# Gates of a gated recurrence: 64-row products with both gates side by side in place of block-diagonal 128-row products

## Chip, cores and metric

One core of a Trainium2 chip runs the whole program. The metric is the device time in microseconds (us) of one execution; lower is better.

## What is computed

One step of a one-layer hybrid decoder over 512 prompt positions and 8 x 4 sample positions (544 tokens). Three branches (GLA, mLSTM, RG-LRU) are fed from one input projection, gated and summed; a convolutional feed-forward part follows. The change touches the gates of the RG-LRU branch only:

```python
def blockdiag(x, w):
    nb, bs, _ = w.shape
    xb = x.reshape(x.shape[:-1] + (nb, bs))
    return jnp.einsum('blnd,nde->blne', xb, w).reshape(x.shape)

# R_WIDTH = 512, R_BLOCKS = 8, so w_rglru_r and w_rglru_i are (8, 64, 64)
r_g = sigmoid(blockdiag(xc, w_rglru_r) + b_rglru_r)
i_g = sigmoid(blockdiag(xc, w_rglru_i) + b_rglru_i)
log_a = R_C * r_g * log_sigmoid(lam)
a = exp(log_a)
bx = sqrt(-expm1(2 * log_a)) * (i_g * xc)
# h[t] = a[t] * h[t-1] + bx[t];   o_r = h * gelu(ry)
```

## The kernel before

Channels lie on partitions, tokens along the free axis. The 512 channels of the RG-LRU branch are four blocks of 128 (i = 0 to 3), and each of them holds two of the 64-channel blocks of the gate weights. A block's row is 568 elements long (512 prompt positions and eight samples with the convolution's padding between).

**The order of the work.** TensorE works through "units": unit u multiplies one 1024 x 128 tile of a weight matrix by all tokens (48 matmuls of 272 columns, L605; each weight is split into a high part `whi` and a low part `wlo`, so three passes). For each unit SyncE loads `stage`, ScalarE copies it into `whi` (L1078), GpSimd subtracts to make `wlo` (L545); ScalarE also copies the unit's product out of PSUM (`gg`, `mo` and others: L1160, L1163). Between the units every engine makes "visits", small pieces of the recurrences, in an order written out by hand in a table (`plan`). Block i of the RG-LRU is `rg` on TensorE and ScalarE and `rgd` on VectorE, behind units 23, 24, 26 and 27; `gfin` (`gv`, `ogh`, `ogl`) stands between block 1 and block 2 on VectorE. TensorE starts unit u only when the product of unit u - 2 has been copied out, and all of them by the end of unit 28, when the gate units begin.

**A block's chain.** VectorE convolves `rx` into `rt[i % 2]` (L1534, L1536, in four steps). TensorE makes the products (L796): `bd` is [128, gate, block, 128], two 64 x 64 gate blocks on the diagonal and zeros beside them. Per block there are four products, two gates times two halves of 284 columns, each into a bank of its own from 4 to 7. ScalarE takes the sigmoid of both gates with their bias from `par` (L1272, L1273), then tanh, exp and sqrt (L1277 to L1279), with two table loads between. VectorE multiplies, scans and multiplies by `ry` (L1816 to L1826, `rg_o`), and splits the result into `orh` and `orl` (L1829, L1830). ScalarE's next block waits for `rg_o` of this one; TensorE's next products wait for this one's sigmoids (`rg_copied`) and for the convolution (`xc`). In ScalarE's queue the next unit's `whi` and copy-out stand behind a block's square root, and GpSimd's `wlo` waits for the `whi`.

**Around it.** `bd` is filled with zeros by GpSimd at the start (L552); SyncE waits for that before it loads the four diagonal parts. `par`, the per-channel biases and gains, is copied out of PSUM by VectorE in two pieces (L1576, L1577), and `cst` is a small tile of 8 columns, of which four are used.

Of the kernel before, what the change touches and what calls it, by code (L numbers as in the profile page):

```python
# [25 lines left out]
ACT = mybir.ActivationFunctionType  # L26
X = mybir.AxisListType.X

P = 128
# [10 lines left out]
CW, FW = 4, 3  # L40
# [21 lines left out]
CONVM = PADM - (CW - 1)  # L62
# [24 lines left out]
P_G2, P_GG, P_MG, P_MCW, P_MCB, P_RCW, P_RCB, P_BR, P_BI, P_LAM = 52, 60, 64, 68, 84, 88, 104, 108, 112, 116  # L87
# [35 lines left out]
def layer(nc, io):  # L123
    ctx = ExitStack()
    with ctx:
        sems = {}

        def s(name):
            if name not in sems:
                sems[name] = ctx.enter_context(nc.semaphore("s_" + name))  # L130
            return sems[name]
# [4 lines left out]
        def at(name, shape, off, dt=F32):  # L136
            return nc.alloc_sbuf_tensor_at(name, shape, dt, offset=BASE + off)
# [13 lines left out]
        o = 71680  # L151
        ident = at("ident", [P, P], o)
        ones = at("ones", [P, P], o + 512)
        par = at("par", [P, PAR_N + KD], o + 1024)
        cst = at("cst", [P, 8], o + 2304)
# [34 lines left out]
        rx = at("rx", [P, 4, PADM], o)  # L190
# [6 lines left out]
        pm = at("pm", [P, 4, PADM], o)  # L197
# [19 lines left out]
        rt = [at(f"rt{i}", [P, PADM], w0 + 12288 + (i + 4) % 6 * 2304) for i in range(6)]  # L217
# [18 lines left out]
        sel = at("sel", [4, H, P], o + 2336)  # L236
        wa2 = at("wa2", [RANK, 2 * P], o + 4384)
        wq = at("wq", [P, 3, H, P], o + 5408)
        bd = at("bd", [P, 2, 4, P], o + 11552)
        ch = at("ch", [P, NB, P], o + 11552)  # L240
        cols = at("cols", [P, 5, 100], o + 15648)
        ecol = at("ecol", [P, 5, 68], o + 17664)
# [61 lines left out]
        def split(ap):  # L304
            return ap.rearrange("p (a b) -> p a b", a=2)
# [3 lines left out]
        def bank(i):  # L309
            return ps[:, i * 512:(i + 1) * 512]  # L310
# [73 lines left out]
        def _(sp):  # L384
# [61 lines left out]
            for n, name in enumerate(("w_mlstm_q", "w_mlstm_k", "w_mlstm_v")):  # L446
                sp.dma_start(wq[:, n], io[name][0].rearrange("h d e -> d h e")).then_inc(s("wq_in"), 16)
            load_all(U_RX, tiles(w_in, C_RX, 8), 8)
            sp.wait_ge(s("zeroed"), 1)
            for n, name in enumerate(("w_rglru_r", "w_rglru_i")):  # L450
                for r in range(2):
                    src = io[name][0].rearrange("(t r) d e -> r d t e", r=2)[r]
                    sp.dma_start(bd[64 * r:64 * r + 64, n, :, 64 * r:64 * r + 64], src).then_inc(s("bd_in"), 16)
            load_all(U_GG, tiles(w_in, C_GG, 4), 4)
            load_all(U_MO, tiles(w_in, C_MO, 4), 4)

# [57 lines left out]
            sem, value = used(U_DOWN - 1)  # L514
# [13 lines left out]
        @block.gpsimd  # L528
        def _(pool):
            done = [0]  # L530

            def then(ins):

                done[0] += 1
                ins.then_inc(s("pool_step"), 1)
                pool.wait_ge(s("pool_step"), done[0])

            def pick(t, op, fill, base, pattern, mult):
                return pool.affine_select(out=t, in_=t, compare_op=op, fill=fill, base=base, pattern=pattern,
                                          channel_multiplier=mult)  # L540

            def lo(u, slot, kt):

                pool.wait_ge(s("hi"), u + 1)
                pool.tensor_tensor(wlo[:, slot, 0:kt], stage[:, slot, 0:kt], whi[:, slot, 0:kt].bitcast(F32),  # L545
                                   ALU.subtract).then_inc(s("lo"), 1)

            then(pool.memset(ident[:], 0.0))
            pick(ident[:], ALU.not_equal, 1.0, 0, [[-1, P]], 1).then_inc(s("ident"), 1)
            for area, value in ((bd[:], 0.0), (ones[:], 1.0), (pm[:, :, 0:CW - 1], 0.0), (rx[:, :, 0:CW - 1], 0.0),  # L550
                                (gst[:], 0.0)):
                pool.memset(area, value).then_inc(s("zeroed"), 1)  # L552
            pool.wait_ge(s("hi"), 1)
            pool.tensor_tensor(wlo[:, 0, :, 0:N_SMALL], stage[:, 0, :, 0:N_SMALL], whi[:, 0, :, 0:N_SMALL].bitcast(F32),
                               ALU.subtract).then_inc(s("lo"), 1)
            lo(1, 1, KT)
            pool.wait_ge(s("lo"), 2)
            pool.memset(qz[0:64, :, 1, :], 0.0).then_inc(s("zeroed"), 1)
            pool.memset(qz[64:P, :, 0, :], 0.0).then_inc(s("zeroed"), 1)
            pool.wait_ge(s("zeroed"), 7)  # L560

            for t, v, fill in ((negm, 0.0, NEG), (cau, 1.0, 0.0)):
                then(pool.memset(t[:], v))
                pick(t[:], ALU.is_ge, fill, 0, [[1, P]], -1).then_inc(s("masks"), 1)
            for t, v, fill in ((negs, 0.0, NEG), (caus, 1.0, 0.0)):
                view = t[:].rearrange("p (b t) -> p b t", t=LS)
                then(pool.memset(t[:], v))
                then(pick(view, ALU.is_ge, fill, 0, [[LS, NB], [1, LS]], -1))
                pick(view, ALU.is_ge, fill, 0, [[-LS, NB], [0, LS]], 1).then_inc(s("masks"), 1)

            then(pool.memset(blk[:], 1.0))
            then(pick(blk[:], ALU.is_ge, 0.0, 0, [[-LS, NB]], 1))
            pick(blk[:], ALU.is_ge, 0.0, LS - 1, [[LS, NB]], -1).then_inc(s("masks"), 1)

            then(pool.memset(blkc[:], 0.0))
            pick(blkc[:].rearrange("p a (b t) -> p a b t", t=LS), ALU.not_equal, 1.0, 0,
                 [[1, NB], [-1, NB], [0, LS]], 0).then_inc(s("masks"), 1)

            then(pool.memset(sel[:], 0.0))
            pick(sel[:], ALU.not_equal, 1.0, 0, [[-1, H], [0, P]], 1).then_inc(s("masks"), 1)  # L580

            lo(2, 2, KT)
            for u0, u1 in ((SLOTS, U_DVE), (U_DOWN, U_END)):
                with pool.Fori(0, (u1 - u0) // SLOTS) as i:
                    for r in range(SLOTS):
                        lo(i * SLOTS + (u0 + r), (u0 + r) % SLOTS, kt_of(u0 + r))

        @block.tensor
        def _(pe):
            mm = nc.tensor.matmul  # L590
# [193 lines left out]
            def v_rg(i):  # L784

                pe.wait_ge(s("xc"), i + 1)
                if i == 0:
                    pe.wait_ge(s("bd_in"), 64)
                    pe.wait_ge(s("ss_new"), 2)
                    pe.wait_ge(s("state_rows"), 2)  # L790
                else:
                    pe.wait_ge(s("rg_copied"), i)
                for w in range(2):
                    for r in range(2):
                        n = CONVM // 2
                        ins = mm(bank(4 + 2 * w + r)[:, 0:n], bd[:, w, i, :], rt[i % 2][:, r * n:(r + 1) * n],  # L796
                                 start=True, stop=True)
                ins.then_inc(s("rg_mm"), 1)

# [182 lines left out]
            for b in range(NB):  # L982
                g, q = divmod(b, FST_BANK)
                ins = tr(bank(4 + g)[:, q * NFR:(q + 1) * NFR], fraw[:, b, :], NFR)
# [3 lines left out]
            for r in range(2):  # L988
                ins = mm(halves(3)[:, r, :], ones[:], ssa[:, r * HT:(r + 1) * HT], start=True, stop=True)
# [29 lines left out]
            for m in range(2):  # L1019
                pe.wait_ge(s("uev"), 2 * NF - 1 + m)  # L1020
                down(m, m, hidden=m == 0)
                if m == 0:
# [4 lines left out]
                    for b in range(1 + NB):  # L1027
                        ins = tr(ps[0:NFR, 2048 + b * P:2048 + (b + 1) * P], rows[:, b * NFR:(b + 1) * NFR], P)
# [18 lines left out]
            for t in range(5):  # L1047
                n = P if t < 4 else TS
                ins = mm(bank(4)[0:n, t:t + 1], yss[:, t * P:t * P + n], ones[:, 0:1], start=True, stop=True)
# [3 lines left out]
        def _(act):  # L1053
            func = nc.scalar.activation
# [211 lines left out]
            def v_rg(i):  # L1266
                act.wait_ge(s("rg_mm"), i + 1)
                if i:
                    act.wait_ge(s("rg_o"), i)
                c0 = CONVM // 2  # L1270
                v = [pair(2 + w).rearrange("p (a b) -> p a b", a=2)[:, :, 0:c0] for w in range(2)]
                func(rt[2][:, 0:CONVM].rearrange("p (a b) -> p a b", a=2), v[0], ACT.Sigmoid, bias=par[:, P_BR + i:P_BR + i + 1])  # L1272
                func(rt[3][:, 0:CONVM].rearrange("p (a b) -> p a b", a=2), v[1], ACT.Sigmoid, bias=par[:, P_BI + i:P_BI + i + 1])\  # L1273
                    .then_inc(s("rg_copied"), 1)
                act.wait_ge(s("rg_copied"), i + 1)
                act.wait_ge(s("c4"), 1)
                then(func(rt[4][:, 0:CONVM], rt[2][:, 0:CONVM], ACT.Tanh, scale=c4[:, i:i + 1]))  # L1277
                func(rt[2][:, 0:CONVM], rt[2][:, 0:CONVM], ACT.Exp, scale=lz[:, i:i + 1])
                func(rt[4][:, 0:CONVM], rt[4][:, 0:CONVM], ACT.Sqrt).then_inc(s("rg_u"), 1)  # L1279
# [122 lines left out]
            for n in range(2 * KD):  # L1402
                u = U_GB + n
                g = PB_GATE + GATE_OF[n // KD] * KD + n % KD
                i, r = divmod(n, 2)
# [20 lines left out]
            for r in range(2):  # L1426
                i = KD // 2 - 1
# [94 lines left out]
        def _(dve):  # L1522
# [48 lines left out]
                v.scalar_tensor_tensor(out=xl[:, j, :], in0=pair(XN_PAIR[j])[:, 0:T], scalar=par[:, P_G1 + j:P_G1 + j + 1],  # L1571
                                       in1=xh[:, j, :].bitcast(F32), op0=ALU.mult, op1=ALU.subtract).then_inc(s("xl"), 1)

            dve.wait_ge(s("zeroed"), 7)
            dve.wait_ge(s("par_tr"), 2)
            v.tensor_copy(par[:, 0:P_LAM + 4], bank(4)[:, 0:P_LAM + 4])  # L1576
            v.tensor_copy(par[:, P:PAR_N], bank(4)[:, P:PAR_N]).then_inc(s("par"), 1)  # L1577
            dve.wait_ge(s("par_tr"), 3)
            for w, dst in enumerate((pm, rx)):
# [592 lines left out]
```

## Time and profile before

| | |
|---|---|
| Median of 3 runs | 1024.71 us (1024.48 to 1026.93) |
| The profiled execution | 1024.34 us |
| Its span, first to last instruction | 1022.3 us |
| TensorE busy | 979.2 us (96%) |
| VectorE busy | 563.2 us (55%) |
| ScalarE busy | 425.0 us (42%) |
| GpSimd busy | 248.2 us (24%) |
| Mean granted TensorE clock | 0.983 |

The profile is of one execution. Busy times are sums over an engine's own instructions; engines work side by side, so the busiest is near the span and the others are not added to it. What lies around the span (2.0 us) belongs to the time but not to the trace.

### The profile page before, as it was taken

Reading aid. Unit: us, or ns where it says so; the run is one execution under the profiler, and the core shown is the slowest. Engines: PE = TensorE matmul, PEld = TensorE weight load, DVE = VectorE, ACT = ScalarE, POOL = GpSimd, SP = SyncE. Lnnn points to the kernel's source line nnn. Section 1 sums busy time; section 2 is a strip of 40 time slices with the busy share of each in tenths; the row PEclk is TensorE's granted clock in tenths of the full one; section 3 lists DMA queues with packets and bytes.
Section 4 is the critical chain, followed back from the end, with each engine's and each line's share of the span. In section 5 each row is a group of like instructions: output and inputs, shape, how many; then the busy total and the mean of one; then the engine's idle time right before and its main releaser. Section 6 shows DMA issues by size and latency. Waiting matters only on the chain.

```text
span 1022.3 us, 19012 instructions
## 1 busy us (share of the span) xinstructions
PE 979.2 (96%) x7594; PEld 953.9 (93%) x7594; DVE 563.2 (55%) x1007; ACT 425.0 (42%) x578; POOL 248.2 (24%) x129
## 2 busy tenths in 40 slices
PE   7999999985899999999999999999999999999995
PEld 6999999884899999888999999999999999999995
DVE  4486336449743345447334577777777777412122
ACT  5642332484544455222232345544554554222221
POOL 3543222313132222222353320000000001334340
PEclk9999999996999999999999999999999999999998
DMA  6243422232122223424421522223322321522212
GB/s 178 71 125 87 109 73 68 67 82 62 42 63 84 63 62 104 121 66 128 135 85 38 139 83 83 83 82 91 94 82 83 100 84 56 141 87 85 84 38 88
DMA packets 159982, 89.38 MB, mean 87 GB/s; under 512 B 6404, under 2 KB 158050, under 8 KB 159929
## 3 DMA queue, kind: packets, MB, share of 16 engines
q1 hardware_dynamic: 144928, 79.16, 27.0%
q10 hardware_dynamic: 15000, 9.47, 3.2%
q8 instruction: 39, 0.64, 0.3%
q14 instruction: 15, 0.12, 0.0%
HBM read 82.29 MB, written 6.32 MB: 87 GB/s over the span
## 4 chain that ended last, share of the span: by engine, by line
PE 84%; DVE 9%; ACT 3%; issue 2%; DMA 0%; ACTq 0%; DVEq 0%
PE ps L605 73%; PE ps L594 4%; PE ps L898 1%; PE ps L817 1%; PE ps L902 1%; PE ps L613 1%; DVE rt L1818 1%; DMA xtok<-x_prompt 0%; PE ps L836 0%; PE ps L832 0%; DVE rt L1822 0%; PE ps L843 0%; DVE omh L1947 0%; PE ps L773 0%; ACT whi L1078 0%
## 5 line engine op out<-in xcount | busy, mean ns | idle before, releaser
L545 POOL TENSOR_TENSOR wlo<-stage,whi 128x1024 fp32r<-128x1024 f32 (+1 forms) x98 | 237.6, 2426 | 733.8 <-ACT whi L1078 733.7
L605 PE MATMUL ps<-xh,whi 128*128 128x272 f32 x1536 | 323.4, 292 | 8.4 <-ACT mo L1163 8.4
L605 PE MATMUL ps<-xh,wlo 128*128 128x272 f32 x1536 | 319.0, 289 | 0.0
L605 PE MATMUL ps<-xl,whi 128*128 128x272 f32 x1536 | 318.2, 289 | 0.0
L605 PEld LDWEIGHTS ps<-xh,whi 128*128 128x128 f32 x1536 | 243.4, 190 | 11.3 <-ACT mo L1163 9.1
L1078 ACT ACTIVATE whi<-stage 128x1024 fp32r<-128x1024 f32 x140 | 146.3, 1045 | 236.9 <-PE ps L605 230.8
L605 PEld LDWEIGHTS ps<-xl,whi 128*128 128x128 f32 x1536 | 243.1, 190 | 0.0
L605 PEld LDWEIGHTS ps<-xh,wlo 128*128 128x128 f32 x1536 | 241.4, 190 | 0.0
L2049 DVE SCALAR_TENSOR_TENSOR ca<-up,par,ca 128x560 f32<-128x560 f32 x88 | 74.1, 842 | 7.6 <-DVE ca L2049 2.7
L605 PE MATMUL ps<-hh,whi 128*128 128x272 f32 x352 | 73.6, 291 | 0.0
L605 PE MATMUL ps<-hl,whi 128*128 128x272 f32 x352 | 72.7, 288 | 0.0
L605 PE MATMUL ps<-hh,wlo 128*128 128x272 f32 x352 | 72.6, 287 | 0.0
L2096 DVE TENSOR_TENSOR yb<-xt,ps 128x544 f32<-128x544 f32 x8 | 5.8, 721 | 106.7 <-PE ps L605 106.7
L605 PEld LDWEIGHTS ps<-hl,whi 128*128 128x128 f32 x352 | 55.6, 188 | 0.0
L605 PEld LDWEIGHTS ps<-hh,wlo 128*128 128x128 f32 x352 | 55.0, 188 | 0.0
L605 PEld LDWEIGHTS ps<-hh,whi 128*128 128x128 f32 x352 | 54.9, 188 | 0.1
L2056 DVE TENSOR_TENSOR wlo<-stage,whi 128x1024 fp32r<-128x1024 f32 x42 | 51.4, 1223 | 0.9 <-ACT whi L1078 0.2
L1400 ACT ACTIVATE sg<-ps,par 128x544 f32<-128x544 f32 x24 | 17.1, 714 | 82.6 <-PE ps L605 77.5
L1449 ACT ACTIVATE hh<-hp 128x512 f32 (+1 forms) x22 | 13.9, 633 | 70.4 <-DVE hp L2078 70.4
L1460 ACT ACTIVATE ca<-up,par 128x560 f32<-128x560 f32 x44 | 37.6, 855 | 6.2 <-DVE up L2032 5.7
L1971 DVE TENSOR_TENSOR sg<-sg,ps 128x544 f32<-128x544 f32 x16 | 11.5, 719 | 49.3 <-PE ps L605 47.3
L1455 ACT ACTIVATE ca<-ca 128x560 f32<-128x560 f32 x22 | 14.8, 672 | 49.9 <-DVE ca L2049 49.9
(416 smaller groups left out, 1324.4 us busy)
## 6 DMA issues: line engine op xcount, KB each, us to landing
stage<-w_in SPq DMA_DIRECT2D x52, 512.0 KB, 3.7
stage<-w_up SPq DMA_DIRECT2D x44, 512.0 KB, 3.7
stage<-w_down SPq DMA_DIRECT2D x16, 512.0 KB, 4.0
stage<-w_branch SPq DMA_DIRECT2D x12, 512.0 KB, 3.3
stage<-w_out SPq DMA_DIRECT2D x8, 512.0 KB, 4.1
stage<-w_down SPq DMA_DIRECT2D x8, 384.0 KB, 3.4
ch<-state_mlstm_C ACTq DMA_DIRECT2D x4, 512.0 KB, 4.9
s_mlstm_C<-ch ACTq DMA_DIRECT2D x4, 512.0 KB, 3.2
```

Of the source, the lines that this page charges most:

```text
L545: pool.tensor_tensor(wlo[:, slot, 0:kt], stage[:, slot, 0:kt], whi[:, slot, 0:kt].bitcast(F32), ALU.subtract).then_inc(s("lo"), 1)
L594: return nc.tensor.transpose(out, in_, ident[0:k, 0:k])
L605: ins = mm(dst[:, r, :], w[:, slot, k0 + step * k, :], x(k)[:, r * HT:(r + 1) * HT], start=first and k == 0 and q == 0, stop=last and k == ...
L613: ins = mm(small_out[0:N_SMALL, c0:c1], w[:, 0, k, 0:N_SMALL], x[:, k, c0:c1], start=k == 0 and q == 0, stop=k == KD - 1 and q == 2)
L1078: func(whi[:, slot, 0:kt], stage[:, slot, 0:kt], ACT.Copy).then_inc(s("hi"), 1)
L1400: func(split(sg[:]), halves(0), ACT.Sigmoid, bias=col).then_inc(s("gate_ev"), 1)
L1449: func(dst[:, 0:SEQ], hp[:, 0:SEQ], ACT.Copy)
L1455: func(ca[:, 0, 0:CONVF], ca[:, 0, 0:CONVF], ACT.Gelu_apprx_tanh).then_inc(s("gelu"), 1)
L1460: func(ca[:, r, 0:CONVF], up[:, r, 0:CONVF], ACT.Identity, bias=par[:, bass.ds(j + (P_FB + NF * r), 1)], scale=par[:, bass.ds(j + (P_FW + ...
L1971: v.tensor_tensor(split(sg[:]), split(sg[:]), halves(1), ALU.mult).then_inc(s("br_mul"), 1)
L2049: v.scalar_tensor_tensor(out=out, in0=row[:, k:k + CONVF], scalar=w, in1=out, op0=ALU.mult, op1=ALU.add)\
L2056: v.tensor_tensor(wlo[:, slot], stage[:, slot], whi[:, slot].bitcast(F32), ALU.subtract).then_inc(s("lo_up"), 1)
```

## The change

Two 64 x 64 gate blocks no longer stand on a diagonal with zeros beside them. `bd` becomes [128, block, 128]: on each half of the partitions both gates of one 64-channel block stand side by side. On partitions 0 to 63 the r gate has columns 0 to 63 and the i gate 64 to 127; on partitions 64 to 127 it is the other way round. A product takes 64 rows of weights and gives both gates of 64 channels. The four products of a block stand in the order (half of the columns, half of the channels). Since a product's result holds one gate on its lower and one on its upper 64 partitions, ScalarE takes the sigmoids in four activations of 64 partitions, and for the i gate it reads one half of the partitions and writes the other. The i gate's bias must lie on the partitions that are read, so VectorE makes a copy of it with the halves exchanged, in `cst` columns 4 to 7. The zero fill and its wait go.

```diff
-        bd = at("bd", [P, 2, 4, P], o + 11552)
+        bd = at("bd", [P, 4, P], o + 11552)
...
-            sp.wait_ge(s("zeroed"), 1)
             for n, name in enumerate(("w_rglru_r", "w_rglru_i")):
                 for r in range(2):
                     src = io[name][0].rearrange("(t r) d e -> r d t e", r=2)[r]
-                    sp.dma_start(bd[64 * r:64 * r + 64, n, :, 64 * r:64 * r + 64], src).then_inc(s("bd_in"), 16)
+                    c0 = 64 * (n ^ r)
+                    sp.dma_start(bd[64 * r:64 * r + 64, :, c0:c0 + 64], src).then_inc(s("bd_in"), 16)
...
-            for area, value in ((bd[:], 0.0), (ones[:], 1.0), (pm[:, :, 0:CW - 1], 0.0), (rx[:, :, 0:CW - 1], 0.0),
+            for area, value in ((ones[:], 1.0), (pm[:, :, 0:CW - 1], 0.0), (rx[:, :, 0:CW - 1], 0.0),
                                 (gst[:], 0.0)):
...
-            pool.wait_ge(s("zeroed"), 7)
+            pool.wait_ge(s("zeroed"), 6)
...
-                for w in range(2):
-                    for r in range(2):
-                        n = CONVM // 2
-                        ins = mm(bank(4 + 2 * w + r)[:, 0:n], bd[:, w, i, :], rt[i % 2][:, r * n:(r + 1) * n],
+                for r in range(2):
+                    for b in range(2):
+                        n, q = CONVM // 2, slice(64 * b, 64 * b + 64)
+                        ins = mm(bank(4 + 2 * b + r)[:, 0:n], bd[q, i, :], rt[i % 2][q, r * n:(r + 1) * n],
                                  start=True, stop=True)
                 ins.then_inc(s("rg_mm"), 1)
...
-                func(rt[2][:, 0:CONVM].rearrange("p (a b) -> p a b", a=2), v[0], ACT.Sigmoid, bias=par[:, P_BR + i:P_BR + i + 1])
-                func(rt[3][:, 0:CONVM].rearrange("p (a b) -> p a b", a=2), v[1], ACT.Sigmoid, bias=par[:, P_BI + i:P_BI + i + 1])\
-                    .then_inc(s("rg_copied"), 1)
+                for b in range(2):
+                    q, other = slice(64 * b, 64 * b + 64), slice(64 - 64 * b, P - 64 * b)
+                    func(split(rt[2][q, 0:CONVM]), v[b][q], ACT.Sigmoid, bias=par[q, P_BR + i:P_BR + i + 1])
+                    ins = func(split(rt[3][q, 0:CONVM]), v[b][other], ACT.Sigmoid, bias=cst[other, 4 + i:5 + i])
+                ins.then_inc(s("rg_copied"), 1)
...
-            dve.wait_ge(s("zeroed"), 7)
+            dve.wait_ge(s("zeroed"), 6)
             dve.wait_ge(s("par_tr"), 2)
             v.tensor_copy(par[:, 0:P_LAM + 4], bank(4)[:, 0:P_LAM + 4])
+            for b in range(2):
+                v.tensor_copy(cst[64 - 64 * b:P - 64 * b, 4:8], bank(4)[64 * b:64 * b + 64, P_BI:P_BI + 4])
             v.tensor_copy(par[:, P:PAR_N], bank(4)[:, P:PAR_N]).then_inc(s("par"), 1)
```

On ScalarE, at block 0 of the RG-LRU (`rt_115` to `rt_117` are `rt[2]` to `rt[4]`; - is before, + is the changed kernel; its line numbers stand two higher from here on):

```order
-L1272 ACT_TABLE_LOAD
-L1272 ACTIVATE rt_115<-ps,par 128x568
-L1273 ACTIVATE rt_116<-ps,par 128x568
-L1277 ACTIVATE rt_117<-rt_115,sml 128x568
+L1274 ACT_TABLE_LOAD
+L1274 ACTIVATE rt_115<-ps,par 64x568
+L1275 ACTIVATE rt_116<-ps,cst 64x568
+L1274 ACTIVATE rt_115<-ps,par 64x568
+L1275 ACTIVATE rt_116<-ps,cst 64x568
+L1279 ACTIVATE rt_117<-rt_115,sml 128x568
```

Two more activations stand ahead of the tanh; the table loads and the rest of the block stay in their places, in the other three blocks too.

On TensorE nothing moves: the four products of a block (now L796 with 64 rows of weights) stand between the same units. On VectorE the two copies of the exchanged bias stand between those into `par`:

```order
L1578 COPY par<-ps 128x120
L1580 COPY cst<-ps 64x4 x2
L1581 COPY par<-ps 128x178
```

Before, nothing stood between the two copies into `par`.

## Rows read from the trace of the kernel before

**Rows 1.** The page: busy tenths and granted clock in 40 equal slices.

```profile
PE   7999999985899999999999999999999999999995
PEclk9999999996999999999999999999999999999998
```

**Rows 2.** Waits of TensorE, 200 to 270 us: total, times, longest us.

```profile
PE ps L796 <- DVE rt L1536: 11.0, 2, 10.3
PE ps L605 <- ACT mo L1163: 8.4, 2, 4.3
```

**Rows 3.** Chain of waits, 180 to 300 us: start us, us, what.

```profile
188.77 6.02 PE ps L605 x48
...
222.55 0.74 ACT rt L1272
...
238.85 2.87 DVE gv L1791 x4
...
250.59 0.75 DVE rt L1816
...
255.42 0.07 ACT rt L1272
```

**Rows 4.** Timeline of TensorE: start us, us, operation, count [idle before]; blocks 0 and 3.

```profile
202.74 2.08 PE L796 MATMUL ps<-rt,bd 128*128 128x284 f32 x8
204.44 0.62 PE L605 MATMUL ps<-xh,whi 128*128 128x272 f32 x2
...
250.60 3.76 PE L796 MATMUL ps<-rt,bd 128*128 128x284 f32 x8 [10.31 <-DVE rt L1536]
```

**Rows 5.** The same timeline, a 64-row product and what follows it.

```profile
194.71 1.98 PE L773 MATMUL ps<-vb,kz 64*128 64x512 f32 x4
196.62 0.52 PE L605 MATMUL ps<-xh,whi 128*128 128x272 f32 x2
```

**Rows 6.** Groups of instructions by form, ScalarE: shapes, count | busy us, mean ns.

```profile
L1231 ACT ACTIVATE ot<-ps 128x512 f32<-128x512 f32 x4 | 2.4, 602 | 0.0
...
L1246 ACT ACTIVATE rout<-ps 27x512 f32<-27x512 f32 x2 | 1.2, 580 | 0.7 <-ACT rout L1246 0.7
```

**Rows 7.** Timeline of ScalarE, block 0.

```profile
208.09 0.73 ACT L1272 ACTIVATE rt<-ps,par 128x568 f32<-128x568 f32 x1
208.72 0.73 ACT L1273 ACTIVATE rt<-ps,par 128x568 f32<-128x568 f32 x1
209.48 0.77 ACT L1277 ACTIVATE rt<-rt,sml 128x568 f32<-128x568 f32 x1
```

**Rows 8.** Timeline of ScalarE, neighbours that read different partitions.

```profile
173.13 0.37 ACT L1234 ACTIVATE ot<-ps 32x256 f32<-32x256 f32 x1 [2.88 <-PE ps L760]
...
173.52 0.38 ACT L1234 ACTIVATE ot<-ps 32x256 f32<-32x256 f32 x1
```

**Rows 9.** Timelines of GpSimd and VectorE before block 2, and L1534 by form.

```profile
245.03 2.67 POOL L545 TENSOR_TENSOR wlo<-stage,whi 128x1024 fp32r<-128x1024 f32 x1 [9.72 <-ACT whi L1078]
...
245.42 2.60 DVE L1534 TENSOR_SCALAR rt<-rx,par 128x568 f32<-128x568 f32 x1
...
L1534 DVE TENSOR_SCALAR rt<-pm,par 128x568 f32<-128x568 f32 x4 | 2.3, 571 | 0.0
```

**Rows 10.** Timeline of TensorE behind two waits; a window's row ends clock, DMA, GB/s.

```profile
231.79 0.82 PE L605 MATMUL ps<-xh,whi 128*128 128x272 f32 x2 [4.12 <-ACT mo L1163]
...
236.87 0.41 PE L605 MATMUL ps<-xh,wlo 128*128 128x272 f32 x2
...
264.67 0.82 PE L605 MATMUL ps<-xh,whi 128*128 128x272 f32 x2 [4.29 <-ACT mo L1163]
...
267.53 0.41 PE L605 MATMUL ps<-xh,whi 128*128 128x272 f32 x2
...
265.00:266.00 1.00, 1.00 (x6) 1.00 (x6) 0.95 (x3) 0.00 (x0) 0.30 (x1) 0.50 0.00 0
```

**Rows 11.** Timeline of VectorE and the chain of waits, start of the program.

```profile
28.40 0.33 DVE L1577 COPY par<-ps 128x178 f32<-128x178 f32 x1
...
35.21 2.02 PE ps L684 x8
```

## Prediction

> **What bounds the kernel now.** The page comes first. TensorE (PE) is busy 96% of the span and its granted clock is near full in all slices but one [rows 1], so over most of the program only TensorE time counts. The tenth slice, from about 230 to 256 us, is the exception (PE busy 5 tenths, clock 6 tenths), and the edited code stands just there. The second view, the waits of TensorE from 200 to 270 us, says how it idles: 11.0 us for the convolution that VectorE makes (L1536) and 8.4 us for ScalarE's `mo` copy-out (L1163) [rows 2], 19.4 us together. The third view, the chain of waits of that stretch, says what sets its length. It is not TensorE. From block 0's sigmoid on, at 208.09 us, the chain goes ScalarE, VectorE, ScalarE, VectorE through the four blocks of the gate recurrence and comes back to TensorE only at 264.67 us [rows 3]: block 0 on ScalarE and VectorE, then block 1 on ScalarE and VectorE, then VectorE's `gv`, `ogh`, `ogl` and the convolution for block 3, VectorE's share of block 2, then ScalarE for block 3, the `whi` copy, a table load and `mo`, for which TensorE waits. Only ScalarE's share of block 2 is off the chain: VectorE starts that block's first step at 250.59 us, straight behind the convolution.
>
> **The products.** Before, each block has four fp32 products over 128 rows of weights, half of them zeros. In block 0 they take 1.70 us from their start to the next unit's (202.74 to 204.44 us), and in block 3 3.76 us, at the lower clock [rows 4]. The number of products stays at four and so does their column count, 284; what falls is the rows, from 128 to 64, with neighbours in the order now on different halves of the array. No row here shows two 64-row products side by side, so their saving is bounded: nothing below, and half above, 0.85 us in each of three blocks at the full clock and 1.9 us in block 3, 4.4 us over all four. I cost it at nothing, whichever it is. In blocks 0 and 1 what hides it is the ScalarE and VectorE chain: TensorE works ahead there and then waits for the convolution [rows 2]. In block 3 ScalarE starts its sigmoid at 255.42 us, after VectorE's L1826, while the products ended at 250.60 + 3.76 = 254.36 us [rows 3, 4]: even unshortened they leave 1.1 us. If this cover were gone, the 4.4 us would be the rival below. A 64-row product between 128-row ones exists already (L773), and what follows it starts 1.91 us later, with no gap around it [rows 5], so switching itself costs nothing that shows. The Trainium skill, TensorEngine Tiling (Array Packing), section Key Properties, says that changing the tiling mode drains TensorE; that speaks against the change, but the rows around L773 leave less than 0.1 us for it, and the sum would be the same by it, as TensorE is idle later in any case.
>
> **The sigmoids: the term that counts.** Two activations of 128 partitions become four of 64 partitions, each over the same 568 elements. ScalarE's time goes with the elements of a partition and not with the partitions: 27x512 takes 580 ns, 128x512 takes 602 ns [rows 6]. So each of the four costs what one costs now, 0.73 us. In the trace the second sigmoid starts 0.63 us after the first and the tanh 0.76 us after the second, 1.39 us from the first sigmoid to the tanh [rows 7]. What two more add depends on whether neighbours still overlap by 0.1 us. If they do, each adds 0.63 us, 1.26 us a block. The only pair in this trace of which the second reads other partitions than the first is L1234's: 0.37 us long, and the second starts 0.39 us after the first [rows 8], so no overlap. In the new code each of the four differs from its neighbour in the start partition of its input or its output. By L1234's row the steps are 0.75 us: three of them and the last 0.76 us are 3.0 us, against 1.39 us, so **+1.6 us a block**. I take that, since it is the pair that has the same trait. The Trainium skill, ScalarE: Activation LUTs, section What ACT_TABLE_LOAD costs, gives back-to-back ACTIVATEs an overlap of about 93 ns and makes no exception; by it each block would pay 1.3 us and the sum below would be 0.9 us less. The table loads stay as they are.
>
> Blocks 0, 1 and 3 have this on the chain: 3 x 1.6 = **+4.8 us**. In block 2 ScalarE's part is done before 245.03 us, when GpSimd's `wlo`, which follows the copy behind that block's square root, starts [rows 9]. Late by three blocks' worth it is done before 249.8 us, while VectorE comes to it at 250.59 + 3.2 = 253.8 us. Hidden there, with 4.0 us left.
>
> **What the shift meets.** VectorE's operations that read SBUF stand still while GpSimd's `wlo` subtraction runs. At that 245.03 us `wlo` starts, and VectorE's L1534, 0.57 us when free, takes 2.60 us [rows 9]. `wlo` moves by 4.8 us (to 249.8 us), but VectorE's convolution, by 3.2 us (to 248.6 us). So it is caught one step later, in the second or third of its four steps. It pays about the same, 2.0 us now against up to 2.4 us (a whole `wlo`), so **+0.2 us**. The collisions in blocks 0, 1 and 3 (L1818) move as a whole, since there `wlo` and VectorE hang on the same square root.
>
> **The clock.** TensorE waits longer before it resumes at about 269.7 us. It resumes at the low clock (0.50, 1.2 GHz) now too: its first six pairs of matmuls, 264.67 to 267.53 us, take 2.86 us; a pair at the full clock takes 0.25 us (a unit of 24 pairs, 6.02 us), so six take 1.5 us, a loss of 1.4 us [rows 3, 10]. After the wait that ended at 231.79 us it was slow for eleven pairs, until 236.87 us, a loss of 2.3 us [rows 10]. Between 0 and +0.9 us, then; I take the middle, **+0.4 us**.
>
> **Edits at nothing.** GpSimd's fill of `bd` with zeros goes, among the first instructions of the program, before its wait for the first `whi`; SyncE's wait for it was met long before SyncE comes there. Two copies of 64x4 into `cst` are added on VectorE ahead of the copy into `par` at 28.40 us; that one, of 128x178, takes 0.33 us, so the two cost 0.7 us at most, and `par` is first needed by TensorE's a2 products at 35.21 us [rows 11]. The product of block i+1 waits for all four sigmoids of block i, but TensorE has idle time behind it in every case.
>
> **The sum.** 4.8 + 0.2 + 0.4 = +5.4 us on the profiled execution's 1024.34 us: 1029.7 us. The median of the runs before stands 0.37 us above it, so **1030.1 us**, 0.5% slower. About 0.3% (3.1 us) is what a measurement of this kernel can tell from no change.
>
> **The rivals.** *Overlap kept* (20%): the four sigmoids stay 0.63 us apart. 3 x 1.26 + 0.2 + 0.4 = +4.4 us, 1029.1 us (with the 0.37 us, as all that follow). For it speaks that the sigmoids overlap now; against it L1234. *The change within the noise* (14%): VectorE's convolution before block 2 slips past `wlo` altogether, which gives 2.0 us back, and the overlap stays: 3.8 - 2.0 = +1.8 us, 1026.5 us. It would have to end before 249.8 us; worked out it ends near 252 us, so this is unlikely, but any 2 us that I don't see in the 62 us of chain would do the same. *TensorE was the bound after all* (6%), the one on the other side: if the waits of TensorE in [rows 2] vanished, say because VectorE meets fewer `wlo` than in this one execution, the chain between 202.7 and 264.7 us would go through the products, the added sigmoids would lie beside TensorE's units, and the 4.4 us would be gained: 1024.34 - 4.4 + 0.37 = 1020.3 us. It decides only from the point where the 19.4 us of waits are gone, and they are now over four times the saving. The Trainium skill, the page named above, section Theoretical Speedup, says up to twice the speed for contractions of 64 rows and less, which is the most that this rival takes from the products' rows. *The products don't overlap* leaves the forecast as it is.
>
> **Numbers.** Forecast 60%, the rivals 20, 14 and 6. Both forecast and first rival are slower by over 0.3%: 80%. Within 0.3%: 14%, faster: 6%. The range takes in the second rival's 1026.5 below. Above, the forecast with the whole clock term (+0.5) and a whole `wlo` (+0.2) is 1030.8 us; one more step of 1.2 us for a collision that I placed wrongly makes 1032.0 us.
>
> **What would show it.** Right: four activations of 64x568 of 0.73 us, 0.75 us apart; tanh 3.0 us behind the first; TensorE resuming after its wait for L1163 at about 269.7 us; TensorE's waits in this stretch longer than 19.4 us by the shift and whatever the products save. Wrong: starts 0.63 us apart, activations of half the length, no wait of TensorE behind block 3, or a chain that runs through L796.

## The result, and the profile after

The changed kernel takes 1029.79 us, the median of 7 runs (1028.03 to 1030.99), against 1024.71 us before (7 runs, 1023.80 to 1026.93): 1.0044 times as long, 95% interval 1.0031 to 1.0056. The profiled execution took 1029.79 us with a span of 1027.8 us; before, 1024.34 and 1022.3 us. So the span grew by 5.5 us, the median by 5.1 us.

The page, the two rows that answer to [rows 1]:

```profile
PE   7999999974799999999999999999999999999995
PEclk9999999996899999999999999999999999999998
```

TensorE is still busy nearly everywhere; the hole around 230 us has become deeper, and the clock is low in part of a second slice. Its waits between 200 and 275 us (total, times, longest, us), against [rows 2]:

```profile
PE ps L605 <- ACT mo L1163: 12.2, 2, 6.3
PE ps L796 <- DVE rt L1538: 10.9, 1, 10.9
PE ps L796 <- ACT rt L1275: 2.9, 2, 2.0
PE ps L605 <- ACT gg L1160: 0.3, 1, 0.3
```

Together 26.3 us instead of 19.4 us. The waits for L1275, the last of the four sigmoids, are new: the sigmoids end later, and TensorE, which comes to the next block's products, finds them not done. ScalarE's block 0 in the timeline (start us, us, operation), against [rows 7]:

```profile
208.28 0.73 ACT L1274 ACTIVATE rt<-ps,par 64x568 f32<-64x568 f32 x1
209.03 0.73 ACT L1275 ACTIVATE rt<-ps,cst 64x568 f32<-64x568 f32 x1
209.77 0.73 ACT L1274 ACTIVATE rt<-ps,par 64x568 f32<-64x568 f32 x1
210.51 0.73 ACT L1275 ACTIVATE rt<-ps,cst 64x568 f32<-64x568 f32 x1
211.27 0.77 ACT L1279 ACTIVATE rt<-rt,sml 128x568 f32<-128x568 f32 x1
```

Four activations of 64 partitions last as long as activations of 128, start 0.74 or 0.75 us apart with no overlap, and the tanh comes 2.99 us behind the first sigmoid instead of 1.39 us. TensorE's timeline, against [rows 4] and [rows 10]:

```profile
203.01 1.23 PE L796 MATMUL ps<-rt,bd 64*128 64x284 f32 x8
204.17 0.52 PE L605 MATMUL ps<-xh,whi 128*128 128x272 f32 x2
...
253.91 2.26 PE L796 MATMUL ps<-rt,bd 64*128 64x284 f32 x8 [10.94 <-DVE rt L1538]
256.10 0.82 PE L605 MATMUL ps<-xh,whi 128*128 128x272 f32 x2
...
269.57 0.82 PE L605 MATMUL ps<-xh,whi 128*128 128x272 f32 x2 [5.87 <-ACT mo L1163]
```

The products are shorter: 1.16 instead of 1.70 us to the next unit's start in block 0, 2.26 instead of 3.76 us to their end in block 3. TensorE resumes behind block 3 at 269.57 us instead of 264.67 us, which is 4.9 us later and nearly the whole loss. The chain of waits shows that ScalarE and VectorE set this, and what was forecast of the collision (columns: start us, us, what):

```profile
225.07 0.73 ACT rt L1275
...
242.21 2.88 DVE gv L1795 x4
...
249.39 0.82 DVE rt L1538
250.23 2.78 DVE rt L1538
253.04 0.82 DVE rt L1538
253.88 0.75 DVE rt L1820
...
259.48 0.73 ACT rt L1275
...
268.81 0.72 ACT mo L1163
269.57 16.72 PE ps L605 x120
```

VectorE's convolution is now caught by GpSimd's `wlo` in its third step (2.78 us) instead of its first [rows 9].

### The profile page after: what moved, and what is told of

Its sections match the earlier page's. It is cut to its first block, busy times and chain, and to the rows that moved or that the text cites. A ratio compares the mean times of both kernels' runs of the same rounds, so it can differ in the third digit from the quotient of the medians.

```text
span 1027.8 us, 19021 instructions
## 1 busy us (share of the span) xinstructions
PE 977.3 (95%) x7594; PEld 951.5 (93%) x7594; DVE 563.7 (55%) x1009; ACT 431.3 (42%) x586; POOL 246.8 (24%) x128
## 4 chain that ended last, share of the span: by engine, by line
PE 85%; DVE 8%; ACT 4%; issue 2%; DMA 1%; ACTq 0%; DVEq 0%
PE ps L605 74%; PE ps L594 3%; PE ps L898 1%; PE ps L817 1%; PE ps L902 1%; DMA xtok<-x_prompt 1%; PE ps L613 1%; DVE rt L1822 1%; DVE rt L1538 0%; ACT rt L1275 0%; PE ps L836 0%; PE ps L832 0%; DVE rt L1826 0%; PE ps L843 0%; ACT L1281 0%
```

## The experiments

Each ran on the chip beside the kernel before, whose median was 1024.64 to 1024.85 us in these series. "Ratio" is to that kernel, with its 95% interval. In the code, `...` stands for what is left out.

**Only the sigmoids halved, old products.**

```diff
-                func(rt[2]..., v[0], ACT.Sigmoid, bias=par[:, P_BR + i:P_BR + i + 1])
-                func(rt[3]..., v[1], ACT.Sigmoid, bias=par[:, P_BI + i:P_BI + i + 1])
+                for w, p0 in ((0, P_BR), (1, P_BI)):
+                    for b in range(2):
+                        q = slice(64 * b, 64 * b + 64)
+                        ins = func(split(rt[2 + w][q, 0:CONVM]), v[w][q], ACT.Sigmoid, bias=par[q, p0 + i:p0 + i + 1])
```

> The kernel before with its 128-row products and its zeros, and only the sigmoids halved: r lower, r upper, i lower, i upper half of the partitions, 64x568 each, so the start partition changes at each of the three steps. My theory (the time of the change is the two added activations of a block, in three of the four blocks): steps of 0.75 us, tanh 3.0 us behind the first sigmoid, +4.8 to +5.4 us against before, about 1029.8 us, as the whole change. Rival (the loss comes from the 64-row products, their switching or a colder TensorE behind them): not above +0.5 us, about 1024.7 us.

Measured: 1030.04 us (5 runs), ratio 1.0050 (1.0037 to 1.0064). The four sigmoids and the tanh in its timeline:

```profile
207.85 2.96 ACT L1275 ACTIVATE rt<-ps,par 64x568 f32<-64x568 f32 x4
210.84 0.77 ACT L1279 ACTIVATE rt<-rt,sml 128x568 f32<-128x568 f32 x1
```

With the 128-row products and the zeros left as they were, the loss is there whole. The rival, that the 64-row products or a colder TensorE cost it, falls.

**Only the products, old sigmoids.** The change without its sigmoids and without the exchanged bias. This kernel leaves out the sorting of the gates, so its recurrence computes something else; it is there for its time alone:

```diff
-                for b in range(2):
-                    q, other = ...
-                    func(split(rt[2][q, 0:CONVM]), v[b][q], ...)
-                    ins = func(split(rt[3][q, 0:CONVM]), v[b][other], ...)
+                func(rt[2]..., v[0], ACT.Sigmoid, bias=par[:, P_BR + i:P_BR + i + 1])
+                func(rt[3]..., v[1], ACT.Sigmoid, bias=par[:, P_BI + i:P_BI + i + 1])
```

> The 64-row products of the change, but two sigmoids of 128 partitions as before, so that each of them takes one gate on the lower and the other gate on the upper half of the partitions with a bias that does not belong to it: the gates are mixed up and the recurrence's result is another. My theory: the products are hidden, 1024.7 us within 0.5 us, with TensorE's waits longer by what the products save (some 3 to 4 us). Rival 1 (TensorE's time counts): 1020.3 us. Rival 2 (64-row products are what costs): 1028 us or more.

Measured: 1025.93 us (11 runs), ratio 1.0008 (0.9999 to 1.0017). TensorE's waits, 200 to 270 us:

```profile
PE ps L796 <- DVE rt L1536: 11.7, 2, 9.9
PE ps L605 <- ACT mo L1163: 9.8, 2, 5.1
```

21.5 us instead of 19.4 us: the waits grew by 2.1 us, less than the 3 to 4 us that I expected, but there is no gain: what the products save is waited away. The median lies 1.2 us above my 1024.7 us, outside the 0.5 us that I gave it, and neither rival is near. The ratio's 0.8 us above before can't be told from nothing by its interval. In the profiled execution TensorE resumes behind block 3 at 264.46 us, against 264.67 us, so this stretch did not lengthen.

**Sigmoids halved in the other order**, by halves of the partitions and not by gates:

```diff
-                for w, p0 in ((0, P_BR), (1, P_BI)):
-                    for b in range(2):
+                for b in range(2):
+                    for w, p0 in ((0, P_BR), (1, P_BI)):
```

> As the run with halved sigmoids and the old products, but in the order r lower, i lower, r upper, i upper: only the middle one of the three steps changes the start partition. If the lost overlap hangs on the start partition: steps 0.63, 0.75, 0.63 us, tanh 2.77 us behind the first sigmoid, 0.24 us a block less than the other order, +0.7 us less in all: about +4.2 to +4.7 us against before. Rival (activations of 64 partitions never overlap): steps of 0.75 us throughout and the same time as the other order, +4.8 to +5.4 us.

Measured: 1029.19 us (5 runs), ratio 1.0038 (1.0024 to 1.0052).

```profile
207.87 0.73 ACT L1275 ACTIVATE rt<-ps,par 64x568 f32<-64x568 f32 x1
...
208.50 0.72 ACT L1275 ACTIVATE rt<-ps,par 64x568 f32<-64x568 f32 x1
...
209.23 0.73 ACT L1275 ACTIVATE rt<-ps,par 64x568 f32<-64x568 f32 x1
...
210.62 0.77 ACT L1279 ACTIVATE rt<-rt,sml 128x568 f32<-128x568 f32 x1
```

The first step, with the same partitions, is 0.63 us, the second, where they change, 0.73 us (the last two steps together 1.39 us), and the tanh comes 2.75 us behind the first sigmoid instead of 2.99 us. The overlap hangs on the start partition, not on the 64 partitions. The rival (no overlap at half width) falls on the trace's rows; the medians, 0.85 us apart, agree, but their intervals overlap. The table at the end of this section shows the 0.7 us in the stretch where it arises.

**Halved in block 2 alone**, the old products:

```diff
+                for w, p0 in ((0, P_BR), (1, P_BI)):
+                    for q in ((slice(0, 64), slice(64, P)) if i == 2 else (slice(0, P),)):
+                        ins = func(split(rt[2 + w][q, 0:CONVM]), v[w][q], ACT.Sigmoid, bias=par[q, p0 + i:p0 + i + 1])
```

> The kernel before, with the sigmoids halved (four of 64x568) in block 2 alone, the block whose ScalarE part I put beside VectorE's gv, ogh, ogl and convolution. My theory: hidden, 1024.7 us within 0.5 us. It shifts GpSimd's wlo by 1.6 us against VectorE's convolution, which it meets all the same. Rival (added ScalarE time counts wherever it is put): +1.6 us, 1026.4 us.

Measured: 1025.19 us (12 runs), ratio 0.9995 (0.9986 to 1.0005). Its VectorE timeline before block 2's first step:

```profile
247.16 0.57 DVE L1535 TENSOR_SCALAR rt<-rx,par 128x568 f32<-128x568 f32 x1
247.76 4.46 DVE L1537 SCALAR_TENSOR_TENSOR rt<-rx,par,rt 128x568 f32<-128x568 f32 x3
252.26 0.75 DVE L1817 TENSOR_TENSOR rt<-rt,rt 128x568 f32<-128x568 f32 x1
```

The same number of added activations costs nothing where VectorE is the later one. The four steps take 5.10 us, against 5.17 us before (245.42 to 250.59 us): the collision with `wlo` moved to a later step and kept its price.

**Each product issued twice**, in the changed kernel:

```diff
-                for r in range(2):
+                for r in (0, 1, 0, 1):
                     for b in range(2):
```

> The changed kernel with each of a block's four products issued twice. My theory (the products lie beside ScalarE's and VectorE's chain): TensorE works 1.2 us more in each of blocks 0 to 2 and up to 2.3 us in block 3, and the time stays at that of the change, 1029.8 us within 0.6 us. In block 3 the products start 4.8 us before ScalarE's sigmoid, so twice 2.2 us just fits. Rival (TensorE's time counts): +4 to +6 us, 1034 us or more.

Measured: 1030.15 us (5 runs), ratio 1.0045 (1.0032 to 1.0058), as the change itself. In its timeline of TensorE block 3's sixteen records take 4.09 us and end 0.7 us ahead of ScalarE's first sigmoid at 260.40 us:

```profile
255.58 4.16 PE L796 MATMUL ps<-rt,bd 64*128 64x284 f32 x16 [11.20 <-DVE rt L1538]
259.67 0.72 PE L605 MATMUL ps<-xh,whi 128*128 128x272 f32 x2
```

From this side too, TensorE's time for the gates counts neither way. One thing is not accounted for: in this execution the 120 matmuls behind the wait took 17.97 us and not 16.72 us, since the clock stayed low for longer (0.50 up to 277 us). Whether the doubled products have to do with it is open.

**The clock behind the wait.** The changed kernel, with work for TensorE while it waits for `mo`:

```diff
+            pe.wait_ge(s("evac"), U_GB - 1)
+            for _ in range(48):
+                tr(bank(3)[:, 384:512], ident[:], P)
             pe.wait_ge(s("evac"), U_GB)
```

> The whole change, with 48 transposes of the identity into a free bank behind unit 28, some 5.3 us of work for TensorE in its wait of 5.9 us, so that it does not go idle there. If the clock that is low behind this wait costs what the rows say (seven slow pairs at 0.45 instead of 0.25 us, 1.4 us), the time is 1.4 us below that of the change, about 1028.4 us, and the first pair behind the wait takes 0.41 us. Rival (transposes don't keep the clock): the same time as the change, 1029.8 us.

Measured: 1027.15 us (10 runs), ratio 1.0020 (1.0009 to 1.0031). TensorE's timeline:

```profile
263.91 5.40 PE L594 MATMUL ps<-ident 128*128 128x128 f32 x48
270.62 0.52 PE L605 MATMUL ps<-xh,whi 128*128 128x272 f32 x2 [1.30 <-ACT mo L1166]
270.97 0.41 PE L605 MATMUL ps<-xl,whi 128*128 128x272 f32 x2
```

The first pair takes 0.52 us, those behind it 0.41 us, and the first 120 matmuls take 15.31 us (chain of waits) instead of 16.72 us, 1.4 us less, as expected. The profiled execution is the slowest of the ten, 1029.40 us, and only 0.4 us below that of the change: it came to this place 1.05 us later (270.62 against 269.57 us), a lag that is there already at block 0's first sigmoid (209.33 against 208.28 us). The medians differ by 2.6 us, more than the 1.4 us; with both intervals about 1 us wide on either side I count the 1.4 us as shown and the rest as open.

**A form of the change without its cost.** Eight products of 64x64 a block, so that each gate lies in its own bank:

```diff
-                for r in range(2):
-                    for b in range(2):
-                        n, q = CONVM // 2, slice(64 * b, 64 * b + 64)
-                        ins = mm(bank(4 + 2 * b + r)[:, 0:n], bd[q, i, :], rt[i % 2][q, r * n:(r + 1) * n],
+                for x in range(2):
+                    for r in range(2):
+                        for b in range(2):
+                            n, q, w = CONVM // 2, slice(64 * b, 64 * b + 64), b ^ x
+                            ins = mm(bank(4 + 2 * w + r)[q, 0:n], bd[q, i, 64 * w:64 * w + 64],
+                                     rt[i % 2][q, r * n:(r + 1) * n],
...
```

The gates' columns stand the same way on both halves of `bd` (`c0 = 64 * n`), and the two old sigmoids are back.

> The change with eight products of 64 rows and 64 columns of weights a block in place of four of 64x128: each gate's two halves come to lie in one bank, so two sigmoids of 128 partitions suffice, as before, and no exchanged bias. No zeros, half the space for the weights. My theory: TensorE's products take as long as the 128-row ones or a little less and are hidden anyway, and the sigmoids have the old length, so the time is that before, 1024.7 us within 0.6 us. Rival (going over to 64-row products costs on its own): 1027 us or more.

Measured: 1024.53 us (12 runs), ratio 0.9992 (0.9983 to 1.0002). Products and sigmoids of block 0:

```profile
202.59 2.13 PE L797 MATMUL ps<-rt,bd 64*64 64x284 f32 x16
204.65 0.52 PE L605 MATMUL ps<-xh,whi 128*128 128x272 f32 x2
```

```profile
207.84 0.73 ACT L1273 ACTIVATE rt<-ps,par 128x568 f32<-128x568 f32 x1
208.48 0.73 ACT L1274 ACTIVATE rt<-ps,par 128x568 f32<-128x568 f32 x1
209.24 0.77 ACT L1278 ACTIVATE rt<-rt,sml 128x568 f32<-128x568 f32 x1
```

The products take 2.06 us, longer than the old ones (1.70 us) and not, as I expected, as long or a little less, and it does not matter; the sigmoids have their old 1.40 us, and so has the kernel its old time. It keeps what the change gains in space (half of `bd`).

**Block 3 later, before and after.** In both kernels:

```diff
-        plan(27, 0, ("rg", 3), ("rgd", 3))
-        plan(28, 0, ("mconv", 0), ("mconv", 1))
+        plan(28, 0, ("rg", 3), ("rgd", 3), ("mconv", 0), ("mconv", 1))
```

> The kernel before with block 3 of the RG-LRU one visit later, behind unit 28 instead of unit 27, so that TensorE and ScalarE have unit 28 and its copy-out behind them and the first gate unit does not wait for block 3's square root. If the chain through ScalarE is what TensorE waits for, TensorE's wait for mo of 4.3 us goes and the first gate unit starts at about 254 us; what is late next is VectorE's mixed product (L1969) behind the first two mLSTM convolutions, at 278 us, so some 3 us are gained: about 1021.7 us. Rival (nothing but VectorE's chain counts): 1024.7 us.

> The changed kernel with block 3 one visit later in the same way. VectorE's chain still carries the four half-width sigmoids of blocks 0, 1 and 3, so I expect the same gain of about 3 us and the same loss of about 5 us: 1026.8 us. Rival: with ScalarE's block 3 no longer in front of the copy-out, block 3's 1.6 us are hidden too: about 1025.2 us.

Measured: 1023.18 us (12 runs), ratio 0.9980 (0.9969 to 0.9992), with the kernel before; 1028.10 us (12 runs), ratio 1.0025 (1.0012 to 1.0037), with the changed one. So 1.5 and 1.7 us are gained, half of what I expected, and the 4.9 us between them stay: the half-width sigmoids cost the same on VectorE's chain. In the two profiled executions block 0's first sigmoid starts at about the same time (209.53 and 209.67 us), TensorE's first matmul behind the mixed product 4.8 us apart (279.91 and 284.71 us). Where the rest went stands in the waits of TensorE, 200 to 300 us, of the kernel before with block 3 later:

```profile
PE ps L795 <- DVE rt L1535: 6.8, 2, 6.1
PE ps L604 <- DVE mix L1968: 5.5, 1, 5.5
PE ps L604 <- ACT mo L1162: 4.1, 1, 4.1
```

The wait behind block 3 is gone, and a new one of 5.5 us for VectorE's mixed product stands in its place.

**Eight products, block 3 later, and work in that new wait**, put together. Beside the two edits above:

```diff
+                    if n == 1:
+                        pe.wait_ge(s("rg_copied"), 4)
+                        for _ in range(44):
+                            tr(bank(5)[:, 384:512], ident[:], P)
```

> Three edits together: eight products of 64x64 a block with full-width sigmoids, block 3 one visit later, and 44 transposes of the identity into a free bank in TensorE's 5.5 us wait for VectorE's mixed product behind the first gate units. From the run with block 3 later (1.5 us below before) the first edit should change nothing, and the transposes should give back the slow pairs behind that wait: 72 matmuls took 10.83 us there instead of 9.02 us, so 1.8 us. Theory: about 3.3 us below before, 1021.4 us. Rival (what the clock gives is taken back by a later wait): 1.5 us below, 1023.1 us.

Measured: 1023.33 us (12 runs), ratio 0.9984 (0.9973 to 0.9996), no better than with block 3 later alone. The chain of waits:

```profile
283.69 2.84 DVE rt L1540
...
286.56 2.84 DVE rt L1540
...
294.66 2.07 PE ps L817 x8
```

TensorE's pairs behind the wait are fast now, but the chain runs through VectorE's mLSTM convolution, which two `wlo` catch, and through ScalarE to the next products (L817). The rival's number was right, its reason only in part. Against the profiled execution with block 3 later alone, the first of these products starts 1.25 us earlier (289.32 against 290.57 us) and the second, behind a wait of 0.33 us for ScalarE, 0.75 us earlier (294.66 against 295.41 us). So a later wait takes back 0.5 us of what the clock gave. At the end 0.3 us is left (1023.25 against 1023.56 us); where the rest went I have not traced. Both this kernel and the one with block 3 later are faster than the kernel before, by 0.2%, and than the changed one.

**The stretch by itself.** A median holds the whole program, with differences between executions that have nothing to do with the gates. The profiled executions show the stretch alone, from the start of block 0's first sigmoid to TensorE's first matmul behind its wait for `mo` behind block 3:

| Kernel | From, us | To, us | Length, us |
|---|---|---|---|
| Before | 208.09 | 264.67 | 56.58 |
| Only the products | 207.87 | 264.46 | 56.59 |
| Eight products | 207.84 | 264.42 | 56.58 |
| Sigmoids halved in block 2 alone | 209.81 | 266.36 | 56.55 |
| Sigmoids halved, the other order | 207.87 | 268.44 | 60.57 |
| Changed | 208.28 | 269.57 | 61.29 |
| Only the sigmoids | 207.85 | 269.17 | 61.32 |
| Changed, products issued twice | 209.94 | 271.24 | 61.30 |
| Changed, with transposes | 209.33 | 270.62 | 61.29 |

The lengths fall into groups that agree within 0.04 us. Halved sigmoids add 4.7 us with old or new products, products shortened or doubled add nothing, and the other order saves 0.7 us, as expected of it.

## Why the prediction was right

**What bounds that stretch** was right: the chain through ScalarE and VectorE, shown from both sides, with the products shortened (no gain) and issued twice (no loss): 56.59 and 61.30 us in the table above, against 56.58 and 61.29 us.

**The products.** The bound of half was not reached: 1.16 us is 0.68 of 1.70 us. It changed nothing, as the term stood at nothing.

**The sigmoids, +1.6 us a block**: 2.99 - 1.39 = 1.60 us. Choosing L1234's pair [rows 8] as the nearest row, against the overlap of the pair that stood in the very place [rows 7], was the choice that carried the number; with the overlap kept it would have been 1.26 us. L1234's pair is a single one and shorter than the sigmoids, so that it would carry over was argued and not shown. The run in the other order shows that the partition is the cause. The Trainium skill, ScalarE: Activation LUTs, section What ACT_TABLE_LOAD costs, gives neighbours an overlap of about 93 ns; where they keep their start partition the rows agree (0.10 us), where it changes they don't.

**Three blocks of four** was right: block 2 alone costs nothing. 3 x 1.60 = 4.8 us against 4.7 us measured up to TensorE's return (4.9 us, of which 0.2 us are there already at the start of the program: unit 1's first matmul at 29.20 instead of 29.02 us). Those 0.2 us don't go with the change: in the run with transposes, which has the whole change, that matmul starts at 28.69 us.

**The collision, +0.2 us**, was of the wrong sign, if of no weight. The four steps took 5.10 us (248.78 to 253.88 us) instead of 5.17 us, while `wlo` ran for 2.40 us and not 2.67 us.

**The clock, +0.4 us**, is the term that no run bears out. At the place that I named it was 0.15 us (16.72 us for 120 matmuls instead of 16.57 us), and even that can't be told from nothing: three kernels in which the stretch up to there has its old length (only the products, eight products, block 2 alone) take 16.84 us. The profiled execution has another 0.5 us on the way to its end (5.5 us in all). It arises in a stretch from 470 to 475 us, where the clock falls (its mean is the third number from the right):

```profile
470.00:475.00 5.00, 4.17 (x24) 3.92 (x25) 3.25 (x5) 1.13 (x3) 0.00 (x0) 0.66 0.40 125
```

In the kernel before, the stretch that answers to it keeps the full clock:

```profile
465.00:470.00 5.00, 4.20 (x35) 4.06 (x36) 3.51 (x6) 1.41 (x4) 0.00 (x0) 1.00 0.52 158
```

TensorE's waits ahead of it, 1.4 and 0.7 us, are the same in both kernels. Ahead of the fall the changed kernel is 5.0 us behind (its six transposes L594 there start at 471.25 against 466.23 us), after it 5.7 us (the next group of them at 560.76 against 555.05 us), of which 0.2 us are made up by the end. The fall does not go with the change: the run with eight products, as fast as the kernel before, has a mean clock of 0.91 from 460 to 480 us, as the changed kernel has, and that with doubled products, as slow as the change, has 1.00.

**Where luck helped.** The sum's 5.4 us and the 5.5 us between the two profiled executions look closer than they are. Of the 5.5 us, 4.7 us are the sigmoids, for which the sum had 4.8 us; 0.2 us from the start and 0.5 us from the later fall of the clock have nothing to do with the change, and they stand where the sum had 0.2 us for the collision and 0.4 us for the clock. The medians, 5.1 us apart, agree with the sigmoid term as well as with the sum.

**Edits at nothing** held. The last copy into `par` starts at 29.04 instead of 28.40 us (0.2 us of that is the later start), and the a2 products start 6.2 us behind unit 1's first matmul in both kernels. The next block's products did wait for the four sigmoids, 2.9 us in all, and the idle time behind them took that up.

**The rivals.** "Overlap kept" fell by the rows of L1274 and L1275, "within the noise" by the interval (its lower end is 1.0031), "TensorE was the bound" by the run with the products alone.

## What to carry to other kernels

Before a product is made cheaper, ask what its new layout asks of the engine that reads it: ScalarE is paid by elements of a partition (0.73 us for 64x568 as for 128x568), so a result that is read 64 partitions at a time costs twice. A saving on an engine that waits is worth nothing, and an addition on one that it waits for is worth its full length, block by block, except where another engine is later. And in a chain of short activations, keep the start partition from one to the next; here that was worth 0.24 us a block.

## What the runs showed that I had not expected

- Two activations in a row overlap by 0.10 us only if input and output start on the same partitions as those of the one in front: steps of 0.63 and of 0.73 to 0.75 us at the same length of 0.73 us. A change of the input's start (with the bias, which moves along) or of the output's alone is enough; the changed kernel has steps of either kind, and all are 0.74 or 0.75 us. The same partitions alone are not enough: the tanh, which reads SBUF and stands behind a wait, starts 0.76 us after a full-width sigmoid.
- Four products of 64 rows on alternating halves of the array take 1.16 us, four of 128 rows 1.70 us, eight of 64x64 2.06 us. No record is shorter than before (399 ns at least, against 400 ns), so I take it that neighbours on different halves overlap in part; no run has two 64-row products on the same half side by side, which would show it.
- The granted clock falls at some waits of one or two microseconds in one execution and not in the next, with the same wait. At about 95 us TensorE waits 2.1 us for ScalarE in the kernel before and 2.2 us in the run with block 2 alone halved; the first keeps a clock of 1.00 from 90 to 100 us, the second 0.83, and starts block 0 of the gates 1.7 us later. This may be much of the spread of a median's single runs (3 us here), though that was only looked at in profiles.
